# Recurrence gates as three split terms in 64-row pairs, with ScalarE reading them block by block

## The reference

```python
def centred_depthwise_conv(u, w, bias):        # CONV_W = 4 taps
    y = up[:, 0:s] * w[0]
    for t in range(1, CONV_W):
        y = y + up[:, t:t + s] * w[t]
    return y + bias

def rg_lru_direction(u, wa, ba, wx, bx, lam, reverse):
    r = sigmoid(block_diag(u, wa, ba))         # 8 blocks of 64 x 64
    i = sigmoid(block_diag(u, wx, bx))
    log_a = -8 * r * softplus(-lam)
    a = exp(log_a)
    mult = sqrt(-expm1(2 * log_a))             # 1 at the first position
    ...                                        # h = a * h_before + mult * i * u, scanned

c = centred_depthwise_conv(u_x, conv_w, conv_b)
h = rg_lru_direction(c, ..., reverse=False) + rg_lru_direction(c, ..., reverse=True)
return h * gelu(u_gate)
```

## Time and profile before

| what | value |
|---|---|
| median of three runs | 1104.51 us |
| the profiled execution's own time | 1103.97 us |
| its span | 1102.2 us |
| TensorE busy | 1079.9 us (98%) |
| VectorE busy | 865.1 us (78%) |
| ScalarE busy | 719.3 us (65%) |
| mixer of layer 0, k = 8 to 48 | about 35 to 178 us |
| the same in layer 1 | about 464 to 606 us |

### The profile page before, as it was taken

How to read it: one execution, slowest core, us unless ns; L and a number is a source line. 1 busy time by engine, 2 the same in 40 slices (tenths; PEclk the granted TensorE clock), 3 DMA queues, 4 the chain that set the end, 5 groups by cost and what they waited for, 6 DMA issues and landing times.

```text
span 1102.2 us, 18335 instructions
## 1 busy us (share of the span) xinstructions
PE 1079.9 (98%) x6419; PEld 939.6 (85%) x6419; DVE 865.1 (78%) x1053; ACT 719.3 (65%) x952; POOL 50.5 (5%) x43
## 2 busy tenths in 40 slices
PE   7999999999999999999999999999999999999996
PEld 6989989988888888998989987788888888888884
DVE  6976885875556556687596768999999999999997
ACT  6466764455454545447766447788888888888874
POOL 1300000000000000210000000000000000000020
PEclk9999999999999999999999999999999999999998
DMA  9955446565665566955445539999999999999981
GB/s 306 245 172 170 118 151 191 159 206 185 195 191 188 186 189 202 245 150 177 134 135 173 162 129 397 396 393 397 394 396 398 392 401 392 400 391 392 377 307 40
DMA packets 151243, 281.71 MB, mean 256 GB/s; under 512 B 26832, under 2 KB 47632, under 8 KB 151184
## 3 DMA queue, kind: packets, MB, share of 16 engines
q1 hardware_dynamic: 146928, 266.69, 70.8%
q0 software_dynamic: 3808, 13.64, 3.3%
q10 hardware_dynamic: 448, 0.59, 0.2%
HBM read 275.11 MB, written 5.77 MB: 255 GB/s over the span
## 4 chain that ended last, share of the span: by engine, by line
PE 83%; DVE 9%; ACT 4%; issue 3%; DMA 0%; DVEq 0%; ACTq 0%
PE ps L1638 22%; PE ps L1640 22%; PE ps L1639 22%; PE ps L1669 6%; PE ps L1671 3%; DVE w_lo L984 3%; PE ps L1859 1%; ACT w_hi L555 1%; PE ps L2087 1%; DVE yl L984 1%; PE ps L1887 1%; ACT p_t L736 1%; PE ps L2004 1%; PE ps L1898 1%; DVE small L1206 1%
## 5 line engine op out<-in xcount | busy, mean ns | idle before, releaser
L984 DVE TENSOR_TENSOR w_lo<-raw,w_hi 128x1024 fp32r<-128x1024 f32 x268 | 327.0, 1234 | 159.1 <-ACT w_hi L555 156.3
L555 ACT ACTIVATE w_hi<-raw 128x1024 fp32r<-128x1024 f32 x268 | 281.0, 1060 | 163.8 <-PE ps L1640 113.9
L1638 PE MATMUL ps<-xx,w_hi 128*128 128x256 f32 x640 | 183.6, 287 | 0.0
L1639 PE MATMUL ps<-xx,w_hi 128*128 128x256 f32 x640 | 181.0, 283 | 0.0
L1640 PE MATMUL ps<-xx,w_lo 128*128 128x256 f32 x640 | 181.0, 283 | 0.0
L1638 PE MATMUL ps<-w_hi,xx 128*128 128x512 f32 x432 | 170.5, 395 | 1.9 <-DVE xx L1025 0.8
L1639 PE MATMUL ps<-w_lo,xx 128*128 128x512 f32 x432 | 168.3, 389 | 0.0
L1640 PE MATMUL ps<-w_hi,xx 128*128 128x512 f32 x432 | 168.2, 389 | 0.0
L984 DVE TENSOR_TENSOR w_lo<-mix,w_hi 128x1024 fp32r<-128x1024 f32 x128 | 152.6, 1220 | 5.0 <-ACT w_hi L555 1.4
L555 ACT ACTIVATE w_hi<-mix 128x1024 fp32r<-128x1024 f32 x128 | 135.1, 1062 | 29.4 <-PE ps L1640 28.9
L1638 PEld LDWEIGHTS ps<-xx,w_hi 128*128 128x128 f32 x640 | 122.7, 192 | 2.3 <-issue 2.1
(11 more groups left out here) (264 smaller groups left out, 1782.2 us busy)
## 6 DMA issues: line engine op xcount, KB each, us to landing
mix<-in_moe_w_gu_dram SPq DMA_DIRECT2D x112, 512.0 KB, 9.9
raw<-in_w_in_dram SPq DMA_DIRECT2D x96, 512.0 KB, 4.2
raw<-in_moe_w_gu_dram SPq DMA_DIRECT2D x80, 512.0 KB, 9.5
mix<-in_moe_w_down_dram SPq DMA_DIRECT2D x80, 512.0 KB, 9.8
raw<-in_ffn_w_gu_dram SPq DMA_DIRECT2D x48, 512.0 KB, 3.7
raw<-in_w_branch_dram SPq DMA_DIRECT2D x24, 512.0 KB, 4.3
raw<-in_ffn_w_down_dram SPq DMA_DIRECT2D x24, 512.0 KB, 3.5
raw<-in_w_out_dram SPq DMA_DIRECT2D x16, 512.0 KB, 4.1
```

The source lines that it names most:

```text
L555: act.activation(halves(u)[0], src, ACT.Copy).then_inc(hi_done, 1)
L984: dve.tensor_tensor(w_l, place(u)[0], w_h.bitcast(F32), ALU.subtract).then_inc(lo_done, 1)
L1638: mm(dst, ah, bh, start=first, stop=False, skip_group_check=True)
L1639: mm(dst, ah, bl, start=False, stop=False, skip_group_check=True)
```

## The change

1. TensorE's gates take three terms in fp32r, like the units: high weights by high input, high by low, low by high. Weights of gate a and gate x of one head stand side by side, so one matmul has 64 rows and 128 columns; 24 matmuls of 256 columns replace 16 in plain float32 (two records each). The two halves hh follow each other on different rows and write different banks.
2. For this the gate weights are split at k = 8: ScalarE copies 128 x 1024 (`wlru_h`), VectorE subtracts 128 x 1024 (`wlru_l`). The convolution's result is split at k = 14: ScalarE `conv_h`, VectorE `conv_l`, 128 x 1024 each. Both use parts of `yh` and `yl` that are free then.
3. The first tap moves from VectorE to ScalarE, k = 9, four instructions from and to SBUF; VectorE's tap 1 waits for it.
4. With the new layout a Tanh of ScalarE covers 64 rows: eight instructions of 64 x 256 at k = at and eight at k = at + 1, in the order of the blocks m instead of the gates. The instruction at +2 waits for both.
5. TensorE's first scores wait only for the first eight of them (banks 4 and 5), the first transposes for the rest.

```diff
@@ scalar engine
+                    if k == AT_CONV:
+                        act.wait_ge(evac_d, evacs(DVE_EVACS, l, 1))
+                        act.wait_ge(evac_a, evacs(ACT_EVACS, l, 1))
...
+                            i = act.activation(conv_t[:, m, :], ux_t[:, m, 0:SEQ], ACT.Identity,
+                                               scale=col[:, w:w + 1], bias=col[:, o:o + 1])
+                        i.then_inc(conv_0, 1)
+                    if k == AT_CONV - 1:
+                        act.wait_ge(wlru_in, 16 * 8 * (l + 1))
+                        act.activation(yhf[:, 2 * D:3 * D], wlru[:, :, :, :, :].rearrange("p d m g o -> p (d m g o)"),
+                                       ACT.Copy).then_inc(wlru_h, 1)
+                    if k == AT_CONV + 5:
+                        act.wait_ge(conv_ok, l + 1)
+                        act.activation(yhf[:, 0:D], cflat, ACT.Copy).then_inc(conv_h, 1)
...
-                            for m in range(BC):
+                            for m, g, hh in itertools.product((2 * (k - at), 2 * (k - at) + 1), range(2), range(2)):
                                 o = (O_HBA, O_HBX)[g] + (2 * l + d) * BC + m
-                                i = act.activation(lru[:, g, SEQ * m:SEQ * m + SEQ],
-                                                   ps[:, 4 + 2 * g + m // 2, SEQ * (m % 2):SEQ * (m % 2) + SEQ],
-                                                   ACT.Tanh, scale=0.5, bias=col2[:, o:o + 1])
+                                bank, c0 = lru_out(m, hh)
+                                q = slice(HD * hh, HD * hh + HD)
+                                i = act.activation(lru[q, g, SEQ * m:SEQ * m + SEQ],
+                                                   ps[HD * g:HD * g + HD, bank, c0:c0 + SEQ],
+                                                   ACT.Tanh, scale=0.5, bias=col2[q, o:o + 1])
                             i.then_inc(lru_tanh, 1)
                         if k == at + 2:
-                            act.wait_ge(lru_tanh, 2 * (2 * l + d) + 1)
+                            act.wait_ge(lru_tanh, 2 * (2 * l + d) + 2)
@@ vector engine
-                    if AT_CONV <= k < AT_CONV + 4:
+                    if AT_CONV < k < AT_CONV + 4:
                         tap = k - AT_CONV
-                        if tap == 0:
...
+                        if tap == 1:
+                            dve.wait_ge(conv_0, l + 1)
...
+                    if k == AT_CONV - 1:
+                        dve.wait_ge(wlru_h, l + 1)
+                        dve.tensor_tensor(ylf[:, 2 * D:3 * D], wlru[:, :, :, :, :].rearrange("p d m g o -> p (d m g o)"),
+                                          yhf[:, 2 * D:3 * D].bitcast(F32), ALU.subtract).then_inc(wlru_l, 1)
+                    if k == AT_CONV + 5:
+                        dve.wait_ge(conv_h, l + 1)
+                        dve.tensor_tensor(ylf[:, 0:D], cflat, yhf[:, 0:D].bitcast(F32), ALU.subtract).then_inc(conv_l, 1)
@@ tensor engine
                                 pe.wait_ge(yb_l, l + 1)
-                                pe.wait_ge(conv_ok, l + 1)
-                                pe.wait_ge(wlru_in, 16 * 8 * (l + 1))
-                            for g in range(2):
-                                for m in range(BC):
+                                pe.wait_ge(wlru_l, l + 1)
+                                pe.wait_ge(conv_l, l + 1)
+                            for m in range(BC):
+                                for n, (w, x) in enumerate(((0, 0), (0, 1), (1, 0))):
                                     for hh in range(2):
+                                        bank, c0 = lru_out(m, hh)
                                         q = slice(HD * hh, HD * hh + HD)
-                                        ins = mm(ps[q, 4 + 2 * g + m // 2, SEQ * (m % 2):SEQ * (m % 2) + SEQ],
-                                                 wlru[q, d, g, m, :], conv_t[q, m, :], start=True, stop=True)
+                                        ins = mm(ps[:, bank, c0:c0 + SEQ], wlru_hl[w][q, d, m, :],
+                                                 conv_hl[x][q, m, :], start=(n == 0 and m % 2 == 0), stop=(n == 2),
+                                                 skip_group_check=True)
...
-                            pe.wait_ge(lru_tanh, 4 * (l + 1))
+                            pe.wait_ge(lru_tanh, 4 * l + 3)
...
+                        if j == 2:
+                            pe.wait_ge(lru_tanh, 4 * (l + 1))
```

More of the change, by code:

```diff
@@ L1 @@
+import itertools
 import math
@@ L174, in build @@
         small = sb("small", [P, 200])
[L175 removed]
+        wlru = sb("wlru", [P, 2, BC, 2, HD])
         rw = sb("rw", [P, KC, E])
```

28 lines of the change are left out of this document (14 added, 14 removed).

## The result

The changed kernel takes 1115.03 us (median of five runs, 1115.0 to 1115.74) against 1104.29 (1103.71 to 1104.66) for the kernel before beside it: a ratio of 1.0102, 95% interval 1.0091 to 1.0114. It is slower by 10.7 us. The forecast was 3.6 us slower, and the range ended at 1110.5. The profiled execution has 1115.43 us of its own time and a span of 1113.6 us.

The account below looks back on a forecast made before the run. The prediction took TensorE to bound each mixer up to the first scores, then VectorE and ScalarE. Later openings of 2.3 (layer 0) and 1.3 us (layer 1) add 3.6 to 1103.97: 1107.6, median 1108.1, range 1105.0 to 1110.5.

Parts of the forecast that it names:

- start of the first gates: TensorE's gates, first direction: 1.36 us later in layer 0 behind VectorE's added subtraction; in layer 1 2.0 us to spare.
- X: Start of the second direction's first Tanh on ScalarE: forecast to move by -0.15 us in layer 0, about -1.1 in layer 1.
- from X to the opening: Second direction, first Tanh to the bias addition opening the softmax chain: 2.42 us longer, through ScalarE's Tanh and VectorE's last split.
- opening: Start of the first bias addition, which opens the softmax chain: +2.3 us in layer 0, +1.3 us in layer 1.
- the two masters: In each mixer TensorE bounds up to the first attention scores, then VectorE and ScalarE for six steps.
- rival C: TensorE's gates: pairs do not run side by side, 3.15 us per direction, +6.0, 1110.5 us; chance 5%.
- The looser wait: TensorE's first scores, waiting for fewer Tanh: does not help, since TensorE is not what is late.
- Rival A: Only TensorE's matmuls count, as a 64-row Tanh takes half the time: -6.4, 1098.1 us; chance 8%.
- Rival B: First direction's lateness is taken up before the scan, for instance by ScalarE's idle times: 0 to +1.5 us; chance 18%.
- Rival D: TensorE's new waits, up to 2.3 us at a time at j = 3, lower its granted clock; chance 4%.
- part 2: ScalarE's gate Tanh: eight more instructions at 0.36 us each, 2.88 us more per direction; upper bound about 0.49 each.
- the first tap's move: VectorE ahead of layer 0's gates: moving tap 0 to ScalarE buys nothing and costs 0.2 us.

Follow-up runs that it names:

- 128 rows, each twice: The kernel before with every gate Tanh issued twice on all 128 rows, the first result into scratch: 1109.22 us.
- 64 rows, half by half: The kernel before with each 128-row gate Tanh split in two, four on rows 0 to 63, then four on rows 64 to 127: 1111.77 us.
- gate by gate: The changed kernel with Tanh batches formed by gate, half 0 of all blocks, then half 1, and first scores waiting for all: 1109.89 us.
- half, gate, block: The changed kernel with each batch's eight Tanh ordered by half written, then gate, then block: 1111.00 us.
- gate, half, block: The changed kernel with each batch's eight Tanh ordered by gate, then half written, then block: 1111.81 us.
- halves alternating: The kernel before with each 128-row gate Tanh issued as two of 64 rows, rows 0 to 63, then 64 to 127: 1117.70 us.

## Why the prediction was wrong in its size

Step by step, in us; "layer 0 / layer 1", with the layer's own shift of 5.75 us taken out of layer 1:

| step | forecast | measured |
|---|---|---|
| start of the first gates | +1.36 / 0 | +0.94 / 0 |
| first direction's first Tanh | -0.6 / -1.46 | -1.05 / -1.46 |
| sixteen Tanh instead of eight | +2.88 | +5.03 |
| taken up before the scan | 0.4 / 0.4 | 0.71 / 0.69 |
| X, second direction's first Tanh | -0.15 / -1.1 | +1.23 / +0.84 |
| from X to the opening | +2.42 | +4.52 / +4.53 |
| opening | +2.3 / +1.3 | +5.75 / +5.37 |

The scan of the first direction, by which the fourth row goes, in VectorE's timeline (after, then before, then both in layer 1):

```profile
94.13 2.27 DVE L1274 TENSOR_TENSOR_SCAN mix<-mix 128x1024 f32<-128x1024 f32 x1
90.86 2.28 DVE L1248 TENSOR_TENSOR_SCAN mix<-mix 128x1024 f32<-128x1024 f32 x1
527.85 2.28 DVE L1274 TENSOR_TENSOR_SCAN mix<-mix 128x1024 f32<-128x1024 f32 x1
519.22 2.28 DVE L1248 TENSOR_TENSOR_SCAN mix<-mix 128x1024 f32<-128x1024 f32 x1
```

**What held.** The direction, and the two masters: the two openings are 11.12 us later in sum, which is nearly the result. The pairs run side by side: twelve pairs start 0.12 us apart (the first two 0.22), from 64.66 to 66.07, as these rows of TensorE's timeline in the changed kernel show, as the earlier trace rows.

```profile
64.66 0.39 PE L1886 MATMUL ps<-yh 64*128 64x256 f32 x2 [1.19 <-DVE yl L1214]
64.88 0.28 PE L1886 MATMUL ps<-yl,yh 64*128 64x256 f32 x2
...
66.07 0.28 PE L1886 MATMUL ps<-yh,yl 64*128 64x256 f32 x2
```

From the first start to the last end that is 66.07 + 0.28 - 64.66 = 1.69 us; the forecast was 1.71. So rival C is out. The delay passes unchanged to the values' matmul (147.62 in the chain of waits against 141.89, 5.73 later). The looser wait buys nothing that the time shows. Rival A is out, since half the rows take the same 0.47 us. Rival B's idle times took up about 0.7 us instead of 0.4, not all. Rival D is out as a cause of the loss. In the profiled execution the busy time by stage has the clock at 1.00 in the same stretch as the earlier trace rows, though TensorE is busy for 30.52 of its 36.60 us only.

```profile
105.30:141.90 36.60, 30.52 (x246) 27.57 (x246) 27.53 (x40) 27.66 (x53) 0.00 (x0) 1.00 0.43 129
```

The fall of the clock itself is real. The kernel whose scores wait for all Tanh has it behind waits of 3.98 and 3.97 us, 0.50 for 3.4 us in each layer, as shown there, and loses nothing by it: it takes 1114.60 us against 1115.03. In the changed kernel three of the five executions have a mean granted clock of 0.992 or 0.993 and the other two 0.996; the three took 1115.00 to 1115.03 us, the two 1115.43 and 1115.74. For these three only the mean is on record, not where the clock fell.

**What failed.** One term, in part 2: "I take 0.36: 8 x 0.36 = 2.88 us more per direction". The step of a Tanh on alternating rows is 0.483 us, so sixteen of them and the lost overlap with the splits add 5.03. The 2.15 us that are missing stand twice in each layer, in X and from X to the opening, and explain the table: in layer 0 the forecast of 2.3, plus 2 x 2.15, less the 0.42 by which the gates started earlier and 0.31 more taken up, is 5.87 against 5.75; in layer 1, 1.3 + 4.3 - 0.29 is 5.31 against 5.37. The 0.42 is in part luck: kernels with the same work ahead of these gates start them between 64.00 and 65.39. (By its own terms the prediction's later start is 1.14 + 0.2 = 1.34, not 1.36.) The prediction had looked for what 64 rows cost for one instruction, and took the overlap of neighbours, which is part of the row of 0.36, to hold for any neighbours. Its upper bound of 0.49 was right by the number, for another reason, but it was not carried into the range: 16 x 0.49 - 8 x 0.36 = 4.96, so 2.08 more in four places, puts the forecast at 1116.4, where the range ended at 1110.5. No rival stood for it.

Two smaller steps: "the first tap's move buys nothing and costs 0.2" does not fit the run without the move, which took 1.9 us longer, though only the 0.39 us in layer 1 are shown to be the tap's; and the idle time ahead of units was not foreseen. The latter adds nothing to the sum, since TensorE is not the master there: the openings alone make up 11.1 of the 11.4 us of span.

## What to carry to other kernels

A fast instruction form is not free if its output has to be read in more instructions: here it gave TensorE 3.67 - 1.69 = 1.98 us per direction, and ScalarE's sixteen instructions for eight cost 5.03 more. Count those on the engine that reads, and ask first whether that engine is on the path behind it. Where an operation must go over halves of the rows, order the instructions so that rows change as seldom as can be, both of what is read and of what is written (where the bias had the same rows): here eight Tanh took 3.85 us with seven changes and 3.10 with one. And where a change gains on one engine and loses on another, apply it only where the losing engine still has idle time ahead of the next join: here the first of two directions, 2.2 us faster than before.

A time may also move because a transfer lands elsewhere, as the start of the first gates may have done here, 64.00 to 65.39 us in kernels in which nothing ahead of it was changed. Before giving a difference to an edit, compare a stretch that starts behind the place where the transfers play in.

## What the runs showed of the hardware

In these runs neighbouring Tanh on ScalarE, 0.47 or 0.48 us long, overlap by about 0.12 us only while their rows stay the same: the step is 0.36 us there and 0.483 where each changes rows. Steps of a 256-column Tanh from PSUM with a bias per row:

| order | changes in a batch of eight | time of eight |
|---|---|---|
| 128 rows, each twice | 0 | step 0.36 |
| 64 rows, half by half | 1 | 3.12 |
| gate by gate | 1 | 3.10 |
| half, gate, block | 3 | 3.36 |
| gate, half, block | 3 | 3.35 |
| halves alternating | 7 | 3.85 |
| block, gate, half (the changed kernel) | 7 | 3.85 |

At the joints with the splits, which cover 128 rows and touch no PSUM: in the changed kernel the split behind a batch, which ends on rows 64 to 127, starts 0.02 us behind its end (66.39 + 3.85 and 70.26), and the next Tanh, on rows 0 to 63, starts 0.02 us behind the split's end (70.26 + 1.06 and 71.34). The Tanh of 128 rows behind the second split starts 0.09 us ahead of its end (75.22 + 1.06 and 76.19). The 64-row Tanh at 71.34 begins on the same row as the split ahead of it, but it reads other rows of PSUM than the last Tanh did, and another number of rows; which of the two costs the overlap there, no run tells.
